# The first microseconds of a two-layer decoder step: memory tokens loaded in two halves, constants loaded later, and the sum of squares moved behind the third key tile

## The chip, the cores and the metric

The kernel runs on one core of one Trainium2 chip. The metric is the device time of one execution in microseconds (us): the median of three runs. TensorE (PE) does the matrix products, ScalarE (ACT) and VectorE (DVE) prepare their operands and read their results, GpSimd (POOL) does some sums, and SyncE (SP) issues most of the loads. The weights are read from device memory as chunks of 128 x 1024 fp32 numbers (512 KB).

## The reference, cut to what matters

One step of a small decoder: a prompt of 256 tokens and 8 samples of 4 tokens (288 token columns in all) go through two layers. Each layer is a recurrent mixer, a cross-attention into 256 memory tokens and a feed-forward part, the last of which has 8 experts. All is in fp32. The piece that the change touches computes the keys and values of the memory tokens:

```
def rms_norm(x, g):
    y = x * rsqrt(mean(x * x, axis=-1) + EPS)
    return y * g

def mem_kv(mem, g, w_k, w_v):          # mem: 256 tokens x 1024 features
    m = rms_norm(mem, g)               # g = norm_memkv[layer]
    k = (m @ w_k).reshape(B, N_MEM, MEM_HEADS, MEM_HD)
    v = (m @ w_v).reshape(B, N_MEM, MEM_HEADS, MEM_HD)
```

## The kernel before, in words

**Tiles.** Activations lie feature-major: 1024 features are `KD` = 8 tiles of 128 partitions, with tokens in the columns. A product of 1024 x 1024 is made of 8 output tiles, each from one weight chunk of eight 128 x 128 blocks. Each fp32 operand is split in two fp32r parts, hi (a copy by ACT) and lo (original minus hi, by DVE), and three matmuls, hi*hi, lo*hi and hi*lo, stand for one product (`mm3`, lines 1773 to 1775). So a key tile of 256 columns is 8 x 3 = 24 matmuls.

**The stream of weights.** SP issues the loads of all chunks in the order in which they are used, into a ring `raw` of 7 places. A place is loaded again once DVE has made the lo part of what was in it (`lo_done`). ACT makes `w_hi` (line 731, in `hi_upto`), DVE makes `w_lo` (line 1137, in `lo_upto`); both have 7 places too, and ACT refills one when PE has finished the group that read it (`full`).

**The order of the work.** `plan()` lists the groups of the whole kernel in order; PSUM's 8 banks go round in that order, so that a group waits until the group that had its bank before has been read by ACT or DVE (`act_freed`, `dve_freed`). The engines' programs are written out by hand in the same order. `AHEAD` says up to which chunk ACT has split weights before it looks at a group.

**The beginning.** SP issues the load of the memory tokens (`memx`, 1 MB), then all small constants (`small`, 984.5 KB: norm weights, convolution weights, identity and other matrices), then three chunks (c0 to c2), the tokens `x_res` (1.2 MB) and four more chunks (c3 to c6). ACT waits for both `memx` and `small`, then multiplies each of the 8 memory tiles with its norm weight (`mem_hi`, line 780), with c0's `w_hi` between them, then makes 8 squares (`memsq`, line 785) and `w_hi` of c1 to c6. DVE makes `mem_lo` (line 1168) and c0's `w_lo`. PE runs key tile 0 on c0, then the group "mem norm" (lines 1820 and 1822): the sum of the squares over the partitions, from `rt`, which POOL adds up from the eight squares (line 2281). Then come key tiles 1 to 7 on c1 to c7, the values (c8 to c15, 192 matmuls of 512 columns, lines 1773 to 1775), and the first mixer's gate products. The factor 1/rms, `rm`, is applied when a key tile is read from PSUM (`kmem`, line 1243), after ACT's root (line 758) and DVE's reciprocal (line 1235). Between key tiles 0 to 3 ACT and DVE make the parts of the second layer's `mem_hi` and `mem_lo` (line 791), between tiles 4 to 7 the squares and parts of the tokens (`h`, `h_hi`, `h_lo`).

## Time and profile before

| | before |
|---|---|
| median of 3 runs | 1945.95 us (1945.78 to 1947.36) |
| span of the profiled execution, first to last instruction | 1944.7 us |
| mean granted TensorE clock in it | 0.973 of full speed |
| PE busy | 1852.8 us, 95% of the span |
| DVE, ACT, POOL busy | 75%, 64%, 10% of the span |
| idle of PE ahead of its first matmul | 14.6 us |
| first chunk's key tile, the idle behind it, "mem norm" | 14.62 to 23.21 us, then 1.73 us |

A row of the timeline gives an instruction's start and duration; consecutive instructions of one kind are merged to one row with their count. PE's matmuls overlap, so what one costs is the distance to the next start, not its duration. A row of the waits gives who idled, what ended the idle time, the total, the number and the longest. "to landing" of a load is the time from its issue to its semaphore. DMA shares are of the core's 16 DMA engines.

### The profile page before, as it was taken

Reading aid. Unit: us, or ns where it says so; the run is one execution under the profiler, and the core shown is the slowest. Engines: PE = TensorE matmul, PEld = TensorE weight load, DVE = VectorE, ACT = ScalarE, POOL = GpSimd, SP = SyncE. Lnnn points to the kernel's source line nnn. Section 1 sums busy time; section 2 is a strip of 40 time slices with the busy share of each in tenths; the row PEclk is TensorE's granted clock in tenths of the full one; section 3 lists DMA queues with packets and bytes.
Section 4 is the critical chain, followed back from the end, with each engine's and each line's share of the span. In section 5 each row is a group of like instructions: output and inputs, shape, how many; then the busy total and the mean of one; then the engine's idle time right before and its main releaser. Section 6 shows DMA issues by size and latency. Waiting matters only on the chain.

```text
span 1944.7 us, 32156 instructions
## 1 busy us (share of the span) xinstructions
PE 1852.8 (95%) x11001; PEld 1601.7 (82%) x11001; DVE 1457.5 (75%) x1765; ACT 1244.2 (64%) x1600; POOL 187.9 (10%) x226
## 2 busy tenths in 40 slices
PE   6998989999899998999999999999999999999994
PEld 6997979999789777978788888888888888888883
DVE  7588456664588568634598988889888898888884
ACT  6576345443476154423687878878788887888873
POOL 3021211000134420201100000000000000000001
PEclk9999999999899999998799999999999999999997
DMA  7646878754443840764799999999999999999993
GB/s 273 227 137 222 327 262 348 268 171 145 155 141 127 310 167 21 277 256 152 281 384 367 380 373 378 360 368 382 372 380 358 374 376 372 383 357 367 381 372 131
DMA packets 150961, 558.35 MB, mean 287 GB/s; under 512 B 16480, under 2 KB 16480, under 8 KB 149424
## 3 DMA queue, kind: packets, MB, share of 16 engines
q1 hardware_dynamic: 139248, 508.71, 70.5%
q10 hardware_dynamic: 6832, 28.44, 3.6%
q0 software_dynamic: 4752, 19.65, 2.8%
q8 instruction: 59, 0.97, 0.2%
q14 instruction: 70, 0.57, 0.1%
HBM read 520.22 MB, written 36.52 MB: 286 GB/s over the span
## 4 chain that ended last, share of the span: by engine, by line
PE 83%; issue 7%; DVE 5%; DMA 2%; ACT 2%; POOL 1%; POOLq 0%; ACTq 0%; DVEq 0%; SPq 0%
PE ps L1773 24%; PE ps L1775 24%; PE ps L1774 24%; DVE w_lo L1137 1%; PE ps L2081 1%; PE ps L2230 1%; DMA raw<-in_stream 1%; PE ps L2208 1%; PE ps L1872 1%; PE ps L1903 1%; DMA y_rows<-ye 1%; PE ps L1894 0%; PE ps L1919 0%; PE ps L2053 0%; ACT w_hi L731 0%
## 5 line engine op out<-in xcount | busy, mean ns | idle before, releaser
L1673 DVE TENSOR_TENSOR w_lo<-raw,w_hi 128x1024 fp32r<-128x1024 f32 x672 | 787.4, 1220 | 49.7 <-ACT w_hi L1062 48.0
L1062 ACT ACTIVATE w_hi<-raw 128x1024 fp32r<-128x1024 f32 x672 | 705.3, 1060 | 142.2 <-PE ps L1775 119.0
L1773 PE MATMUL ps<-w_hi,xe_hi 128*128 128x512 f32 x896 | 358.2, 400 | 4.7 <-DVE w_lo L1673 4.7
L1775 PE MATMUL ps<-w_hi,xe_lo 128*128 128x512 f32 x896 | 354.5, 396 | 0.0
L1774 PE MATMUL ps<-w_lo,xe_hi 128*128 128x512 f32 x896 | 354.0, 395 | 0.0
L731 ACT ACTIVATE w_hi<-raw 128x1024 fp32r<-128x1024 f32 x212 | 220.5, 1051 | 164.3 <-PE ps L1775 109.8
L1137 DVE TENSOR_TENSOR w_lo<-raw,w_hi 128x1024 fp32r<-128x1024 f32 x212 | 266.9, 1268 | 71.7 <-ACT w_hi L731 70.7
L1773 PE MATMUL ps<-h_hi,w_hi 128*128 128x288 f32 x928 | 278.4, 300 | 7.0 <-DVE h_lo L1164 4.2
L1774 PE MATMUL ps<-h_lo,w_hi 128*128 128x288 f32 x928 | 274.5, 296 | 0.0
L1775 PE MATMUL ps<-h_hi,w_lo 128*128 128x288 f32 x928 | 273.6, 295 | 0.0
L1773 PEld LDWEIGHTS ps<-w_hi,xe_hi 128*128 128x128 f32 x896 | 168.9, 189 | 43.0 <-DVE w_lo L1673 5.0
L1775 PEld LDWEIGHTS ps<-w_hi,xe_lo 128*128 128x128 f32 x896 | 168.7, 188 | 40.1
L1774 PEld LDWEIGHTS ps<-w_lo,xe_hi 128*128 128x128 f32 x896 | 169.0, 189 | 38.3
L1773 PEld LDWEIGHTS ps<-h_hi,w_hi 128*128 128x128 f32 x928 | 174.4, 188 | 15.7 <-issue 14.1
L1773 PE MATMUL ps<-w_hi,gt_hi 128*128 128x512 f32 x448 | 178.1, 398 | 0.0
L1775 PE MATMUL ps<-w_hi,gt_lo 128*128 128x512 f32 x448 | 176.9, 395 | 0.0
L1774 PE MATMUL ps<-w_lo,gt_hi 128*128 128x512 f32 x448 | 176.9, 395 | 0.0
L1775 PEld LDWEIGHTS ps<-h_hi,w_lo 128*128 128x128 f32 x928 | 175.4, 189 | 0.0
L1774 PEld LDWEIGHTS ps<-h_lo,w_hi 128*128 128x128 f32 x928 | 175.0, 189 | 0.3
L1775 PEld LDWEIGHTS ps<-w_hi,gt_lo 128*128 128x128 f32 x448 | 84.2, 188 | 20.0
L1774 PEld LDWEIGHTS ps<-w_lo,gt_hi 128*128 128x128 f32 x448 | 84.3, 188 | 19.4
L1773 PEld LDWEIGHTS ps<-w_hi,gt_hi 128*128 128x128 f32 x448 | 84.2, 188 | 19.3
(411 smaller groups left out, 2551.3 us busy)
## 6 DMA issues: line engine op xcount, KB each, us to landing
raw<-in_experts SPq DMA_DIRECT2D x672, 512.0 KB, 5.5
raw<-in_stream SPq DMA_DIRECT2D x253, 512.0 KB, 4.5
rest<-in_stream SPq DMA_DIRECT2D x28, 512.0 KB, 7.3
x_rows<-zeros ACTq DMA_DIRECT2D x1, 13824.0 KB, 59.6
out_ssd_s<-s_new ACTq DMA_DIRECT2D x16, 512.0 KB, 6.8
y_rows<-ye POOLq DMA_DIRECT2D x9, 512.0 KB, 7.2
home<-in_stream SPq DMA_DIRECT2D x8, 512.0 KB, 7.5
xs<-x_rows POOLq DMA_DIRECT2D x8, 512.0 KB, 4.7
```

What stands on the lines that cost most here:

```text
L731: act.activation(w_hi[:, o % HL, :], landing_place(k), ACT.Copy).then_inc(hi_done, 1)
L1062: act.activation(w_hi[:, (NSPLIT + p) % HL, :], raw[:, slot, :], ACT.Copy) \
L1137: dve.tensor_tensor(w_lo[:, o % HL, :], landing_place(k), w_hi[:, o % HL, :].bitcast(F32), ALU.subtract).then_inc(lo_done, 1)
L1673: dve.tensor_tensor(w_lo[:, (NSPLIT + p) % HL, :], raw[:, (NRING + p) % RAW, :], w_hi[:, (NSPLIT + p) % HL, :].bitcast(F32), ALU.subtract) \
L1773: pe.matmul(out, l_hi, r_hi, start=start, stop=False)
L1774: pe.matmul(out, l_hi, r_lo, start=False, stop=False)
L1775: return pe.matmul(out, l_lo, r_hi, start=False, stop=stop)
L1872: a = pe.matmul(out[:, tt * NMEM:(tt + 1) * NMEM], q[:, j, tt * P:(tt + 1) * P], kt[:, j, :], start=(dd == 0), stop=(dd == 1))
L1903: a = pe.matmul(out, vt[:, m, j * P:(j + 1) * P], prt[:, m, j // 2, :], start=(m == 0), stop=(m == 1))
L2081: a = pe.matmul(out[:, j * n:(j + 1) * n], adt_s[half][0:n, tt, 4 * hb + j:4 * hb + j + 1].broadcast_to([n, n]), tri_r[:, :], start=(j == ...
L2208: a = pe.matmul(ps[:, j // 4, (j % 4) * P:(j % 4 + 1) * P], htok[0:n, m, j * P:(j + 1) * P], sel0[0:n, m, :], start=(m == 0), stop=(m == 2))
L2230: a = pe.transpose(ps[:, 4, k * P:(k + 1) * P], ge[:, f % 2, k * P:(k + 1) * P], ident)
```

## The change

- The memory tokens and the norm weights of their keys and values, which were a part of `small`, are now one input array. It is loaded in two halves: the weights of both layers with memory tiles 0 to 3, and tiles 4 to 7.
- SP's order is now: first half, c0, second half, c1, c2, `small`, c3, `x_res`, c4 to c6.
- ACT runs a square root of one column at its very start, behind a memset by DVE. The table of functions for the root is so loaded before anything has landed; the activations Identity, Square and Copy are in it too.
- ACT no longer waits for `small` ahead of the memory tiles. c0's `w_hi` comes behind memory tile 0 (it came behind tile 3), and c1's behind tile 7 (it came behind the squares). DVE makes c0's `w_lo` behind tile 0 (it came behind tile 4), and c1's behind tile 5.
- PE runs "mem norm" behind key tile 2, not 0. It is the third place later in `plan()` too, which moves it two banks on, and lets ACT split c7 and c8 ahead of the root, and DVE c6 and c7 ahead of the reciprocal.
- `small` is 16 columns shorter, so that all buffers that lie behind it start 64 bytes earlier.

The core of the diff:

```
-for _name, _n in [("g_mix", 16), ("g_mem", 16), ("g_memkv", 16), ("g_ffn", 16),
+for _name, _n in [("g_mix", 16), ("g_mem", 16), ("g_ffn", 16),
...
+NORM_BEHIND = 3
...
-    p = second(memory(0), "mem norm")
+    first = memory(0)
+    p = first[:NORM_BEHIND] + [("mem norm", "act", 0)] + first[NORM_BEHIND:]
...
-            sp.dma_start(memx[:, :, :], t["mem"]).then_inc(mem_in, 16)
-            sp.dma_start(small[:, :], t["small"]).then_inc(small_in, 16)
+            sp.dma_start(memx_g[:, 0:MEM_HALF], t["mem"][:, 0:MEM_HALF]).then_inc(mem_in[0], 16)
...
+                if i == 0:
+                    sp.dma_start(memx_g[:, MEM_HALF:], t["mem"][:, MEM_HALF:]).then_inc(mem_in[1], 16)
                 if i == 2:
+                    sp.dma_start(small[:, :], t["small"]).then_inc(small_in, 16)
+                if i == 3:
                     sp.dma_start(x[:, :, :], t["x"]).then_inc(x_in, 16)
...
-            act.wait_ge(mem_in, 16)
-            act.wait_ge(small_in, 16)
+            act.wait_ge(warm, 1)
+            act.activation(rmt[:, 0:1], rm[:, 0:1], ACT.Sqrt)
+            act.wait_ge(mem_in[0], 16)
             for j in range(KD):
+                if j == 1:
+                    hi_upto(1)
+                if j == KD // 2:
+                    act.wait_ge(mem_in[1], 16)
                 act.activation(mem_hi[0][:, j, :], memx[:, j, :], ACT.Identity,
-                               scale=gains("g_memkv", 0)[:, j:j + 1]).then_inc(hh_done, 1)
-                if j == 3:
-                    hi_upto(1)
+                               scale=mem_gains(0)[:, j:j + 1]).then_inc(hh_done, 1)
+            hi_upto(2)
             for j in range(KD):
                 act.activation(memsq[:, j, :], memx[:, j, :], ACT.Square).then_inc(sq_done, 1)
+            act.wait_ge(small_in, 16)
             root("mem norm", rmt, NMEM + 2)
...
-            dve.wait_ge(small_in, 16)
+            dve.memset(rm[:, 0:1], 1.0).then_inc(warm, 1)
             for j in range(KD):
-                scaled_lo(mem_lo[0], memx, gains("g_memkv", 0), mem_hi[0], j, j + 1)
-                if j == 4:
+                scaled_lo(mem_lo[0], memx, mem_gains(0), mem_hi[0], j, j + 1)
+                if j == 0:
                     lo_upto(1)
+                if j == 5:
+                    lo_upto(2)
+            dve.wait_ge(small_in, 16)
             act_read("mem norm")
...
-                    if l == 0 and j == 0:
+                    if l == 0 and j == NORM_BEHIND - 1:
+                        pe.wait_ge(small_in, 16)
                         out = open_group("mem norm", NMEM + 2)
                         pe.wait_ge(acc_done, KD - 1)
...
-            pe.wait_ge(small_in, 16)
             keys(0, range(KD))
```

What SP issues first. Before, and then in the changed kernel (`memx_g` is the array with the norm weights in its first 16 columns):

```order
L661 DMA memx<-in_mem 128x2048
L662 DMA small<-in_small 128x1969
L695 DMA raw<-in_stream 128x1024 x3
L697 DMA x_res<-in_x 128x2304
L695 DMA raw<-in_stream 128x1024 x4
```

```order
L670 DMA memx_g<-in_mem 128x1040
L703 DMA raw<-in_stream 128x1024
L705 DMA memx_g<-in_mem 128x1024
L703 DMA raw<-in_stream 128x1024 x2
L707 DMA small<-in_small 128x1953
L703 DMA raw<-in_stream 128x1024
L709 DMA x_res<-in_x 128x2304
L703 DMA raw<-in_stream 128x1024 x3
```

The constants moved from the second place to behind c2, and c0 from the third to the second, behind half the memory.

What ACT runs first, up to the root of the norm. Before, and then changed (`landed0` is the semaphore of the ring's first place):

```order
L780 ACT_TABLE_LOAD [waits small_in]
L780 ACTIVATE mem_hi_72<-memx,small 128x256 [waits mem_in]
L780 ACTIVATE mem_hi_72<-memx,small 128x256 x3
L731 ACTIVATE w_hi<-raw 128x1024 [waits landed0]
L780 ACTIVATE mem_hi_72<-memx,small 128x256 x4
L785 ACTIVATE memsq<-memx 128x256 x8
L731 ACTIVATE w_hi<-raw 128x1024 [waits landed1]
...
L758 ACT_TABLE_LOAD
L758 ACTIVATE rmt<-ps,small 128x258 [waits full]
```

```order
L790 ACT_TABLE_LOAD
L790 ACTIVATE rmt<-rm 128x1 [waits warm]
L797 ACTIVATE mem_hi_72<-memx_g 128x256 [waits mem_in0]
L743 ACTIVATE w_hi<-raw 128x1024 [waits landed0]
L797 ACTIVATE mem_hi_72<-memx_g 128x256 x3
L797 ACTIVATE mem_hi_72<-memx_g 128x256 [waits mem_in1]
L797 ACTIVATE mem_hi_72<-memx_g 128x256 x3
L743 ACTIVATE w_hi<-raw 128x1024 [waits landed1]
L801 ACTIVATE memsq<-memx_g 128x256 x8
L743 ACTIVATE w_hi<-raw 128x1024 [waits landed2,small_in]
...
L743 ACTIVATE w_hi<-raw 128x1024 [waits full,landed0]
L743 ACTIVATE w_hi<-raw 128x1024 [waits full,landed1]
```

Two table loads became one that waits for nothing, the split of c0 moved ahead by three tiles and that of c1 ahead of the squares, and two more splits (c7 and c8, the last two rows) stand ahead of the root, which follows them.

What DVE runs up to the reciprocal. Before, and then changed:

```order
L1168 SCALAR_TENSOR_TENSOR mem_lo_74<-memx,small,mem_hi_72 128x256 [waits hh_done,small_in]
L1168 SCALAR_TENSOR_TENSOR mem_lo_74<-memx,small,mem_hi_72 128x256 [waits hh_done] x4
L1137 TENSOR_TENSOR w_lo<-raw,w_hi 128x1024 [waits hi_done]
L1168 SCALAR_TENSOR_TENSOR mem_lo_74<-memx,small,mem_hi_72 128x256 [waits hh_done] x3
L1137 TENSOR_TENSOR w_lo<-raw,w_hi 128x1024 [waits hi_done] x5
L1235 RECIPROCAL rm<-rmt 128x258 [waits act_freed]
```

```order
L1246 MEMSET rm 128x1
L1185 SCALAR_TENSOR_TENSOR mem_lo_74<-memx_g,mem_hi_72 128x256 [waits hh_done]
L1154 TENSOR_TENSOR w_lo<-raw,w_hi 128x1024 [waits hi_done]
L1185 SCALAR_TENSOR_TENSOR mem_lo_74<-memx_g,mem_hi_72 128x256 [waits hh_done] x5
L1154 TENSOR_TENSOR w_lo<-raw,w_hi 128x1024 [waits hi_done]
L1185 SCALAR_TENSOR_TENSOR mem_lo_74<-memx_g,mem_hi_72 128x256 [waits hh_done] x2
L1154 TENSOR_TENSOR w_lo<-raw,w_hi 128x1024 [waits hi_done,small_in]
L1154 TENSOR_TENSOR w_lo<-raw,w_hi 128x1024 [waits hi_done] x5
L1255 RECIPROCAL rm<-rmt 128x258 [waits act_freed]
```

c0's `w_lo` moved ahead by four tiles; c1's stands between tiles 5 and 6 of `mem_lo`; the wait for the constants stands behind them all, and eight chunks are split ahead of the reciprocal, not six. From the fourth key tile on, and on all engines, the rows of the two kernels are the same but for their line numbers, the name of the memory's array and the bank waits of two groups of the values.

## Rows read from the trace of the kernel before

**Rows 1.** The page, its first line

```profile
span 1944.7 us, 32156 instructions
```

**Rows 2.** Waits of PE, whole span: total us, times, longest

```profile
PE ps L1820 <- POOL rt L2281: 3.8, 1, 3.8
```

**Rows 3.** The chain that ended last, first 15 us: start, us, what

```profile
1.44 7.02 DMA small<-in_small
...
8.53 1.28 ACT L780
...
9.82 1.70 ACT mem_hi L780 x4
```

**Rows 4.** Windows: us, busy (x) of PE, PEld, DVE, ACT, POOL; clock, DMA, GB/s

```profile
14.60:18.60 4.00, 3.98 (x19) 4.00 (x20) 3.17 (x4) 4.00 (x10) 3.26 (x5) 1.00 1.03 411
...
26.00:28.70 2.70, 2.70 (x14) 2.70 (x14) 2.66 (x5) 2.13 (x4) 0.00 (x0) 0.50 0.93 278
...
30.00:47.00 17.00, 17.00 (x143) 17.00 (x143) 14.94 (x24) 13.88 (x26) 6.90 (x7) 1.00 0.53 174
```

**Rows 5.** Loads with KB, us to landing: memory, chunk c0

```profile
memx<-in_mem SPq DMA_DIRECT2D x1, 1024.0 KB, 4.8
...
raw<-in_stream SPq DMA_DIRECT2D x1, 512.0 KB, 7.8
```

**Rows 6.** Timeline of SP and ACT from the start: start, us, engine, line

```profile
0.99 0.39 SPq L661 DMA_DIRECT2D memx<-in_mem  x1
...
1.91 1.68 SPq L695 DMA_DIRECT2D raw<-in_stream  x3
...
11.43 1.04 ACT L731 ACTIVATE w_hi<-raw 128x1024 fp32r<-128x1024 f32 x1
...
13.97 2.55 ACT L785 ACTIVATE memsq<-memx 128x256 f32<-128x256 f32 x8
16.42 5.78 ACT L731 ACTIVATE w_hi<-raw 128x1024 fp32r<-128x1024 f32 x6
```

**Rows 7.** Timeline of DVE, 10 to 28 us

```profile
13.31 1.22 DVE L1137 TENSOR_TENSOR w_lo<-raw,w_hi 128x1024 fp32r<-128x1024 f32 x1
14.44 2.23 DVE L1168 SCALAR_TENSOR_TENSOR mem_lo<-memx,small,mem_hi 128x256 fp32r<-128x256 f32 x3
17.50 7.87 DVE L1137 TENSOR_TENSOR w_lo<-raw,w_hi 128x1024 fp32r<-128x1024 f32 x5 [0.83 <-ACT w_hi L731]
25.63 1.77 DVE L1235 RECIPROCAL rm<-rmt 128x258 f32<-128x258 f32 x1 [0.25 <-ACT rmt L758]
```

**Rows 8.** Timeline of PE: first matmul, norm, tile 1, values, gate

```profile
14.62 0.55 PE L1773 MATMUL ps<-mem_hi,w_hi 128*128 128x256 f32 x1 [14.62 <-DVE w_lo L1137]
...
23.21 1.22 PE L1820 MATMUL ps<-rt,small 128*128 128x256 f32 x2 [3.75 <-POOL rt L2281]
...
24.94 0.56 PE L1773 MATMUL ps<-mem_hi,w_hi 128*128 128x256 f32 x1
...
46.86 0.40 PE L1773 MATMUL ps<-w_hi,mem_hi 128*128 128x512 f32 x1
...
68.65 0.29 PE L1773 MATMUL ps<-h_hi,w_hi 128*128 128x288 f32 x1
```

**Rows 9.** Timeline of POOL: the sum of squares of the memory

```profile
14.76 0.75 POOL L2281 TENSOR_TENSOR rt<-memsq 128x256 f32<-128x256 f32 x1 [14.06 <-ACT memsq L785]
15.66 7.50 POOL L2281 TENSOR_TENSOR rt<-rt,memsq 128x256 f32<-128x256 f32 x6
```

**Rows 10.** Timeline of DVE, key tile 5's step, beside POOL's second sum

```profile
41.30 0.42 DVE L1243 TENSOR_TENSOR kmem<-ps,rm 128x256 f32<-128x256 f32 x1 [0.47 <-PE ps L1775]
41.64 1.56 DVE L1168 SCALAR_TENSOR_TENSOR h_lo<-x_res,small,h_hi 128x288 fp32r<-128x288 f32 x2
43.12 1.83 DVE L1137 TENSOR_TENSOR w_lo<-raw,w_hi 128x1024 fp32r<-128x1024 f32 x1
```

**Rows 11.** Window of the experts, columns as in rows 4

```profile
1100.00:1944.00 844.00, 818.91 (x3658) 663.35 (x3656) 728.81 (x674) 664.77 (x694) 12.54 (x19) 0.99 0.95 358
```

More of the change, by code:

```diff
@@ L306, in build_program @@
         assert dt_off + 2880 <= end, (dt_off + 2880, end)
-        memx = at("memx", [KD, NMEM], F32, S[5])
+        memx_g = at("memx_g", [2 * KD + KD * NMEM], F32, S[5])
+        memx = memx_g[:, 2 * KD:].rearrange("p (k n) -> p k n", n=NMEM)
+        MEM_HALF = 2 * KD + KD // 2 * NMEM
         memsq = at("memsq", [KD, NMEM], F32, S[3])
@@ L450, in build_program @@
         x_in = sem("x_in")
-        mem_in = sem("mem_in")
+        mem_in = [sem(f"mem_in{i}") for i in range(2)]
+        warm = sem("warm")
         prev_in = sem("prev_in")
@@ L634, in landing_place, with mem_gains @@
             return rest[:, n, :] if kind == "split" else raw[:, n % RAW, :]
+        def mem_gains(l):
+            return memx_g[:, l * KD:(l + 1) * KD]
         def bank(g, n=512, rows=P):
@@ L791, in _ @@
                         act.activation(mem_hi[1][:, k, :], memx[:, k, :], ACT.Identity,
-                                       scale=gains("g_memkv", 1)[:, k:k + 1]).then_inc(hh_done, 1)
+                                       scale=mem_gains(1)[:, k:k + 1]).then_inc(hh_done, 1)
                 else:
@@ L1226, in conv_tile @@
                                          ALU.mult, ALU.add).then_inc(done, 1)
+            dve.memset(rm[:, 0:1], 1.0).then_inc(warm, 1)
+            for j in range(KD):
+                scaled_lo(mem_lo[0], memx, mem_gains(0), mem_hi[0], j, j + 1)
+                if j == 0:
+                    lo_upto(1)
+                if j == 5:
+                    lo_upto(2)
             dve.wait_ge(small_in, 16)
-            for j in range(KD):
-                scaled_lo(mem_lo[0], memx, gains("g_memkv", 0), mem_hi[0], j, j + 1)
-                if j == 4:
-                    lo_upto(1)
             act_read("mem norm")
@@ L1248, in _ @@
                     if j < 4:
-                        scaled_lo(mem_lo[1], memx, gains("g_memkv", 1), mem_hi[1], k, KD + k + 1)
+                        scaled_lo(mem_lo[1], memx, mem_gains(1), mem_hi[1], k, KD + k + 1)
                     else:
@@ L2473, in small_inputs @@
     put("g_mem", gains(a["norm_mem"]))
-    put("g_memkv", gains(a["norm_memkv"]))
     put("g_ffn", gains(a["norm_ffn"]))
@@ L2592 @@
         "x": feature_major(np.concatenate([a["x_prompt"][0], a["x_sample"].reshape(NB * TS, D)])),
-        "mem": feature_major(a["mem_prompt"][0]),
+        "mem": np.ascontiguousarray(np.concatenate(
+            [a["norm_memkv"].reshape(2 * KD, P).T, feature_major(a["mem_prompt"][0]).reshape(P, KD * NMEM)], 1)),
         "g_fin": np.ascontiguousarray(np.broadcast_to(a["norm_final"][None], (P, D))),
```

## The prediction

> **What bounds the kernel now.** I read the waits of PE first. Over the whole span PE works nearly all the time, and the change touches only its beginning, so the question is what PE waits for there. Two waits stand out: the first matmul starts at 14.62 us, after c0's lo part [rows 8], and "mem norm" waits 3.8 us for POOL's sum of squares [rows 2]. Then the chain of waits tells what lies ahead of 14.62: the constants land at 1.44 + 7.02 = 8.46 us, the table load takes 1.28, ACT's memory tiles follow from 9.82 [rows 3], c0 is split at 11.43 by ACT [rows 6] and at 13.31 by DVE [rows 7]. c0 itself had landed at 1.91 + 7.8 = 9.7 us [rows 5, 6]. So the start hangs on the constants, on a table and on an order of ACT and DVE, not on the weights. Behind the second wait there is a third cost, which no wait shows. PE's clock fell in the idle time: between 26.0 and 28.7 us it is granted 0.50 (1.2 GHz), and 14 matmuls start in 2.7 us, one in 0.19 to 0.21; from 30 to 47 us it is 1.00 (2.4 GHz), and 143 start in 17 us, one in 0.119 [rows 4]. In the first 4 us of work the row shows 1.00 but 19 matmuls in 4.0 us [rows 4]: the pace, 0.21, is that of the lower level, and I go by the pace. A key tile of 24 matmuls takes 24 x 0.119 = 2.86 us at the upper level. The values start at 46.86 us [rows 8]; that is the mark by which I measure the head start.
>
> **The loads.** The memory's 1.05 MB, issued at 0.99, landed 4.8 us later, at 5.8 [rows 5, 6], and the queue moves 411 GB/s while it is full [rows 4]. The transfers came one behind the other: the constants' 1.01 MB would add 2.5 us to 5.8, and landed at 8.46; c0 another 1.3, and landed at 9.7. In the new order, with 1.3 us for each 0.52 MB: first half at 4.5 us, c0 at 5.9 (a tenth added, as both rows above came a tenth or two late), second half 7.2, c1 8.5, c2 9.7, constants 12.2, c3 13.5, the tokens 16.4, c4 17.7, c5 18.9, c6 20.2. c7 and c8 are issued as c0 and c1 are done with, while the queue is still full, and land at 21.5 and 22.8. Nothing is added or removed but one issue by SP (0.4 us, ahead of c1, which has over 6 us until it lands: nothing). The Trainium skill (DMA: Bandwidth & Descriptors, section Specifications) gives a limit of about 358 GB/s from device memory per core. By it the first half and c0, 1.06 MB, would come 0.4 us later than at 411, and the head start would be 0.4 us shorter; the trace has 411 and does not agree, and I go by the trace.
>
> **Table load and start of PE.** The table load (1.28 us [rows 3]) waits only for the engines' start, and with DVE's memset and one activation of one column (bounds: nothing, and the 0.5 us of a whole memory tile) is over by about 3 us, ahead of 4.5. I take nothing. Where the load is gone from at 22 us it lay beside POOL's sum: nothing too. ACT does memory tile 0 at 4.6, waits for c0 (5.9), and splits it in 1.04 us [rows 6]. DVE follows with 1.22 [rows 7], free since 5.5: lo part done at 8.2, PE starts at 8.3 us. Before, 14.62. **Gain 6.3.**
>
> **Tile 0.** PE then needs the memory tiles' lo parts. ACT resumes at 6.9, a tile each 0.40 us (four from 9.82 to 11.43 [rows 3, 6]), the second half has landed, and tile 7 is done at 9.8. DVE takes tiles 1 to 5 from 8.1 to 10.2, a tile each 0.42, while PE uses one in 3 x 0.21 = 0.63 us: no wait up to tile 5, whose matmuls end at 8.3 + 18 x 0.21 = 12.1. But now c1's lo part stands ahead of tiles 6 and 7. ACT splits c1 from 9.7 to 10.8, and makes the squares from 10.7. POOL begins its sum at about 11.4, and beside POOL DVE is slower: three memory tiles took 2.23 us, 0.74 each, with one of them at the undisturbed pace [rows 7], so up to 0.9 each; five weight splits took 7.87, 1.57 each instead of 1.22 [rows 7]. So c1's lo part is done at 12.3, tile 6 at 13.1 and tile 7 at 14.0. PE waits 1.0 and 0.5 us and ends tile 0 at 14.5: 6.2 us for what took 23.21 - 3.75 - 14.62 = 4.8 [rows 8]. **Loss 1.4.** The bounds: without POOL's slowing tile 7 is there at 12.9 and the loss is 0.3; with a fully slowed c1 (1.8 us, as in [rows 10]) it is 1.9. I take 1.4, which is nearest to the rows.
>
> **The wait of 3.75 us.** POOL's seven additions took 14.76 to 23.16, 8.4 us [rows 9]. From 11.4 that is 19.8 at the latest. PE runs tiles 1 and 2 first, 14.5 + 2 x 2.86 = 20.2. c1's parts are there at 12.3; c2's at 15.9, since ACT's eight squares end at 13.1 (2.55 us [rows 6]) and its split and DVE's take 1.0 and 1.7; needed at 17.4. The constants, which PE, ACT and DVE now await ahead of the norm, land at 12.2: ACT is behind its squares until 13.1, so a margin of 0.9 us. The wait goes to nothing, with 0.4 us to spare: **gain 3.8** (bounds 3.4 and 3.8).
>
> **The clock behind it.** Without the idle time PE stays at the upper level. "mem norm", 23.21 to 24.94, takes half of 1.73: **gain 0.9**. Tile 1 ended six tiles ahead of 46.86, at 46.86 - 6 x 2.86 = 29.7, so it took 4.8 us from 24.94; now 2.86: **gain 1.9**. Without the clock's return in time the two are nothing, and tiles 1 and 2 cost up to 2 us each more.
>
> **Tiles 3 to 7 and the values.** c3 to c7 are split by ACT as they land (c4 17.7, c5 18.9, c6 20.2, c7 21.5) and by DVE 2.2 to 3 us behind: 20, 21.5, 22.7, 23.9 for c4 to c7. PE needs c4 at 24.0, c5 at 26.8, c7 at 32.5. The root on ACT is now behind the split of c8 (landed 22.8, done 23.8), so it ends at 24.2, and DVE's reciprocal (1.77 us [rows 7]) at 26.0. Before, that ended at 27.4 with one key tile done; now it has five behind it. So DVE starts reading key tiles with a backlog. A step of DVE takes some 2.4 us, and beside POOL's second sum 44.88 - 41.30 = 3.6 us (0.34 + 1.48 + 1.76 by the starts [rows 10]). By these, c8's lo part is done at 30.7, c9's 33, c10's 37, c11's 40.5, c12's 43.5. The values take them from 35.4 on, one in 2.7 us (eight from 46.86 to 68.65 before [rows 8]): c11 at 43.6, c12 at 46.3. The margin is 2.8 us at the least, so I cost the backlog at nothing. The banks too: tile 7 needs tile 0's bank read (26.4, against 32.5). Everything behind starts from landings, semaphores and ring places that move along with PE.
>
> **The sum.** 6.3 - 1.4 + 3.8 + 0.9 + 1.9 = 11.5; walked along PE: 14.5, 20.2, norm until 21.1, five tiles until 35.4, against 46.86: 11.4. The profiled span, 1944.7 [rows 1], becomes 1933.3. The median of the runs lies 1.25 us above that span, so I predict **1934.5 us**.
>
> **The rivals.**
> *DVE is not slowed (a larger gain).* Tiles 6 and 7 come at the undisturbed pace, and the loads land a little earlier: 12.4 to 13 us, 1933.3. For it: POOL's first additions are short and DVE may slip between them. Against: 2.23 us for three tiles.
> *The clock comes late.* PE's start has now two holes of 1.0 and 0.5 us in it. In the profile it reached the upper pace about 4 us after its unbroken start, and 5.5 us after 23.21. If it comes only at some 18 us, tile 1 and a part of tile 2 run at half pace: 1.8 us lost, up to 3.5 if it takes the tile behind too; 1936.3 to 1938.
> *The loads don't come one by one.* If the first half and c0 share the queue with what is behind, c0 lands 1 to 3 us later and so does PE's start: 1937. This is also the case in which the change doesn't do what it says. The Trainium skill (DMA: Bandwidth & Descriptors, section Queues, rings and completion order) says that completion is not FIFO per issuing engine, which would speak for it. The landings 5.8, 8.46 and 9.7, in the order of issue and spaced by their sizes, speak against.
> *Given back in the values.* If DVE is beside POOL in all of tiles 0 to 7, four more steps cost 1.2 each, c11's lo part comes at 45.3, and PE waits 1.7 us there; 9.7 of the gain stay. That alone is still faster; only if the backlog grows by some 10 us is the gain within 0.2%, 1943, and the chance below is for that.
> *Slower.* The experts' stretch, 844 us at a DMA share of 0.95 and PE at 97% [rows 11], is close to both limits. The buffers behind the constants lie 64 bytes lower, the experts' operands among them. If that made each of the 672 expert chunks dearer by over (11.4 + 3.9) / 672 = 0.023 us, the kernel would be slower by over 0.2%; at 0.03 us, 1955. Nothing in the rows says that an address counts.
>
> **How the numbers follow.** Forecast 0.60; larger gain 0.10; clock late 0.14; loads not one by one 0.07; given back 0.06; slower 0.03. About 0.2%, 3.9 us, is what can be told from no change. The first four are all faster by more: 0.91; given back is the same: 0.06; slower 0.03. The range reaches from the larger gain, with half a us for the runs' spread, to the late clock: 1932.6 to 1938.5. It leaves out the end of the late loads, the fifth and the sixth case, some 0.15.
>
> **What would show it.** In the profile after: first matmul at 8.3 us and the last of the eight memory tiles' matmuls at 14.5; no wait on POOL ahead of the norm; granted clock 1.00 and a pace of 0.119 from tile 1 on; the values from 35.4 us; every later mark, the experts' start too, 11 us earlier. The steps are wrong if c0 lands after 7 us, if tile 6 does not wait, if tile 1 is at 0.21, or if DVE's lo parts end PE's waits in the values.

## The result: 0.5% faster, and the profile after

| | before | after |
|---|---|---|
| median | 1948.87 us (22 runs) | 1943.89 us (22 runs) |
| ratio of the runs, 95% interval | | 0.9948 (0.993 to 0.9965) |
| profiled execution, its span | 1945.95, 1944.7 us | 1929.92, 1928.3 us |
| mean granted clock in it | 0.973 | 0.977 |
| executions below 1940 us | 0 | 7 |
| executions from 1940 to 1951 us | 17 | 13 |
| executions from 1951 to 1961 us | 5 | 1 |

The change is faster, as forecast, but by 5 us, not by 11.5, and the median lies outside the range. (Five executions took from 2073 to 3684 us and are left out of all that is sorted and counted below: one of after, one of experiment 10, and three of before taken beside experiments 8 to 11; without its one, after's median is 1943.63.) The medians alone mislead. Sorted, the executions of each kernel fall into two groups. Before: 17 from 1945.8 to 1950.9 (median 1948.5), 5 from 1956.7 to 1960.7 (1958.1). After: 7 from 1929.9 to 1937.5 (1935.4), 14 from 1942.2 to 1951.2 (1945.4). Group against group the gain is 13.1 and 12.7 us. The medians are only 5 us apart since before's lies in its lower group and after's in its upper one. The three runs on which the prediction stood were all of before's lower group.

**The beginning.** First, what PE waits for in the first 60 us of after (total us, times, longest):

```profile
PE ps L1793 <- DVE w_lo L1154: 8.5, 1, 8.5
PE ps L1793 <- DVE mem_lo L1185: 1.1, 2, 0.9
```

The start and two short holes are all. The wait of [rows 2] on POOL is gone. Then the landings of the first 20 us (KB, us from issue to landing), the memory's two halves and the constants, and the piece of the chain of waits that is c0's load:

```profile
memx_g<-in_mem SPq DMA_DIRECT2D x1, 520.0 KB, 3.9
memx_g<-in_mem SPq DMA_DIRECT2D x1, 512.0 KB, 5.9
small<-in_small SPq DMA_DIRECT2D x1, 976.5 KB, 9.2
...
1.44 4.72 DMA raw<-in_stream
```

With their issues (0.99, 1.90 and 3.52 us) they landed at 4.9, 7.8 and 12.7 us, and c0 at 6.2: one behind the other, in the order of issue, each 0.3 to 0.6 us later than forecast. The timeline of ACT and DVE up to the reciprocal, and of POOL's sum, which answers to [rows 6, 7, 9] (start, duration, engine, line, [idle before, released by]):

```profile
0.99 1.28 ACT L790 ACT_TABLE_LOAD   x1 [0.99 <-PEq L2618]
2.29 0.20 ACT L790 ACTIVATE rmt<-rm 128x1 f32<-128x1 f32 x1
4.89 0.51 ACT L797 ACTIVATE mem_hi<-memx_g 128x256 fp32r<-128x256 f32 x1 [2.40 <-DMA memx_g<-in_mem]
6.17 1.06 ACT L743 ACTIVATE w_hi<-raw 128x1024 fp32r<-128x1024 f32 x1 [0.77 <-DMA raw<-in_stream]
...
7.26 1.23 DVE L1154 TENSOR_TENSOR w_lo<-raw,w_hi 128x1024 fp32r<-128x1024 f32 x1 [1.34 <-ACT w_hi L743]
...
11.01 1.22 DVE L1154 TENSOR_TENSOR w_lo<-raw,w_hi 128x1024 fp32r<-128x1024 f32 x1 [0.54 <-ACT w_hi L743]
12.15 1.83 DVE L1185 SCALAR_TENSOR_TENSOR mem_lo<-memx_g,mem_hi 128x256 fp32r<-128x256 f32 x2
...
11.67 1.14 POOL L2301 TENSOR_TENSOR rt<-memsq 128x256 f32<-128x256 f32 x1 [10.97 <-ACT memsq L801]
12.96 6.79 POOL L2301 TENSOR_TENSOR rt<-rt,memsq 128x256 f32<-128x256 f32 x6
```

The table is loaded and the root run by 2.5 us, beside the loads. c0 is split as it lands. The two memory tiles beside POOL take 1.83 us, 0.92 each. POOL ends at 19.75. PE's timeline, which answers to [rows 8]:

```profile
8.54 0.58 PE L1793 MATMUL ps<-mem_hi,w_hi 128*128 128x256 f32 x1 [8.54 <-DVE w_lo L1154]
...
13.15 0.39 PE L1793 MATMUL ps<-mem_hi,w_hi 128*128 128x256 f32 x1 [0.85 <-DVE mem_lo L1185]
...
14.04 0.38 PE L1793 MATMUL ps<-mem_hi,w_hi 128*128 128x256 f32 x1 [0.26 <-DVE mem_lo L1185]
...
14.48 0.28 PE L1793 MATMUL ps<-mem_hi,w_hi 128*128 128x256 f32 x1
...
19.92 0.64 PE L1841 MATMUL ps<-rt,small 128*128 128x256 f32 x2
...
20.77 0.36 PE L1793 MATMUL ps<-mem_hi,w_hi 128*128 128x256 f32 x1
...
34.47 0.39 PE L1793 MATMUL ps<-w_hi,mem_hi 128*128 128x512 f32 x1
```

First matmul at 8.54, tile 1 at 14.48, norm at 19.92 without a wait, values at 34.47 against 46.86 [rows 8]. The head start is 12.4 us, forecast 11.4. So the beginning did what was predicted, and the missing microseconds had to be sought far behind it.

### The profile page after: what moved, and what is told of

Read it like the earlier page. It is cut to its first block, busy times and chain, and to the rows that moved or that the text cites. A ratio compares the mean times of both kernels' runs of the same rounds, so it can differ in the third digit from the quotient of the medians.

```text
span 1928.3 us, 32159 instructions
## 1 busy us (share of the span) xinstructions
PE 1842.7 (96%) x11001; PEld 1589.5 (82%) x11001; DVE 1456.7 (76%) x1766; ACT 1243.0 (64%) x1600; POOL 187.2 (10%) x226
## 4 chain that ended last, share of the span: by engine, by line
PE 82%; issue 7%; DVE 5%; DMA 3%; ACT 2%; POOL 0%; POOLq 0%; ACTq 0%; DVEq 0%; SPq 0%
PE ps L1793 24%; PE ps L1794 24%; PE ps L1795 24%; DVE w_lo L1154 1%; PE ps L2250 1%; PE ps L2101 1%; DMA raw<-in_stream 1%; PE ps L2228 1%; PE ps L1892 1%; PE ps L1923 1%; DMA out_ssd_s<-s_new 1%; DMA y_rows<-ye 1%; PE ps L1914 0%; ACT w_hi L743 0%; PE ps L1939 0%
```

## The experiments

In all profiles the mark is the start of the values, the first matmul with 512 columns. A head start is its distance from before's 46.86.

**1. The changed kernel again (a_again).** No edit.

> The changed kernel, unaltered, once more, to see in which stretches an execution of about 1944 us differs from the profiled one of 1929.9. Theory 1 (the head start of 11.4 us is real and is carried to the end; what varies between executions is how long TensorE is granted the lower clock later on): executions come in two groups some 11 us apart, near 1933 and near 1945, with mean granted clocks near 0.976 and 0.970; in a profile of the upper group the values start at 35 us as in the fast one, and the lost time lies in one or two stretches of granted 0.50 behind 800 us. Rival 1 (the head start itself is lost in some executions, by late loads or a late clock in the first key tiles): in a profile of the upper group the values start near 46 us, and the later stretches are alike. Rival 2 (the experts' chunks take longer in some executions, from the 64 bytes): the stretch of the experts is longer at a clock of 1.00.

Nine runs: five from 1931.5 to 1935.3 and four from 1942.5 to 1948.9; ratio 0.9917 (0.9887 to 0.9947). The profile taken was this time of the upper group, span 1947.3 at a clock of 0.968. Its beginning is nearly that of after (values at 36.13, a head start of 10.7), and yet it ends 19 us later than after's. The two groups are of one and the same kernel, and the difference is not made at the beginning. There a_again shows one thing that after doesn't, POOL's sum and the norm:

```profile
13.19 7.71 POOL L2301 TENSOR_TENSOR rt<-rt,memsq 128x256 f32<-128x256 f32 x6
...
21.05 0.67 PE L1841 MATMUL ps<-rt,small 128*128 128x256 f32 x2 [0.72 <-POOL rt L2301]
```

The six additions took 7.71 us, not 6.79, and PE waits 0.72 us for them. In the later profiles with the changed beginning they took 7.5 to 7.8, and PE waited 0.5 to 0.7 where it had not waited longer already; after's is the exception. The last addition makes the difference. In after it started at 19.01, just ahead of VectorE's split of c3 (19.20), and took 0.74 us. In a_again that split came first, at 19.09, and the addition, from 19.23, took 1.67:

```profile
L2301 POOL TENSOR_TENSOR rt<-rt,memsq x1: 1672/1672/1672, 19.2 to 19.2; 128x256 f32<-128x256 f32 x1
```

Theory 1 of the expectation holds but for the place: the lost time lies near 690 us, not behind 800 (see "Where the groups part").

**2. The first load held back (a_late).** SP waits for a memset by DVE of 2048 columns ahead of its first load:

```
+            sp.wait_ge(held, 1)
...
+            dve.memset(kmem[0][:, :, :], 0.0).then_inc(held, 1)
```

> The changed kernel with the first load held back by a memset of one 128 x 2048 tile on VectorE, 1 to 2.5 us, so that everything behind starts later by d and nothing else changes. Theory 1 in the form that the later clock losses depend on when idle times fall, counted from the start: the two groups shift by d only, but the share of executions in the upper group changes from that of the unaltered kernel (14 of 21). Rival 1 and 2: the groups shift by d, and the share stays. If the groups are d later and the share is the same within what 5 rounds can tell, the theory of timing from the start is not supported.

```profile
10.87 0.58 PE L1796 MATMUL ps<-mem_hi,w_hi 128*128 128x256 f32 x1 [10.87 <-DVE w_lo L1156]
...
37.70 0.39 PE L1796 MATMUL ps<-w_hi,mem_hi 128*128 128x512 f32 x1
```

PE's timeline: first matmul 2.3 us later than in after, values at 37.70, which is 1.6 later than in a_again. Twelve runs: 1937.43, ten of them from 1934.8 to 1940.5 with a median of 1937.1. That is 1.8 above after's lower group and 3.7 above that of a_again, measured beside it. Inside a group a later start is carried to the end, as far as such scatter lets one say. Only two of the twelve were in the upper group, against four of nine in a_again; so few executions don't settle whether the start's time sets the share.

**3. The sum behind tile 0 again (a_norm1).**

```
-NORM_BEHIND = 3
+NORM_BEHIND = 1
```

> The changed kernel with the norm's sum back behind the first key tile; loads, table and split orders stay. By the steps of the prediction PE starts at 8.5 us and ends tile 0 at 14.5, then waits for POOL until 19.8 (5.3 us, longer than before, since the start moved by 6.1 and the sum by only 3.1), the clock falls, the norm takes 1.7 and tile 1 up to 4.8: the values start at about 19.8 + 1.7 + 4.8 + 17.2 = 43.5 us, 3.4 earlier than before, 8 later than in the changed kernel. So 1945 in the lower and 1953 in the upper group if theory 1 holds and the clock falls; if the clock does not fall in that wait, 41 us and 2 us less. Rival 1: no difference to the changed kernel beyond its scatter.

```profile
20.92 1.19 PE L1841 MATMUL ps<-rt,small 128*128 128x256 f32 x2 [6.15 <-POOL rt L2301]
...
43.44 0.39 PE L1793 MATMUL ps<-w_hi,mem_hi 128*128 128x512 f32 x1
...
16.00:26.20 10.20, 5.28 (x23) 5.13 (x24) 7.18 (x7) 6.18 (x9) 4.35 (x4) 0.50 1.03 411
```

Two rows of PE's timeline and one window (columns as in [rows 4]): PE waits 6.15 us for POOL, the clock is at 0.50 for the 10.2 us from 16.0, and the values start at 43.44, a head start of 3.4. So of the 10.7 us of a_again, 7.3 hang on the new place of the sum. Without it most of the earlier start goes into a longer wait for POOL. Twelve runs: 1952.96, ratio 0.9994 (0.9968 to 1.002), so the rest of the change alone does not move the median. Four are from 1940.1 to 1944.7 (median 1941.6, expected 1945), eight from 1950.9 to 1956.8 (1955.6, expected 1953). Against before's groups measured beside it, 1948.1 and 1958.8, they gain 6.5 and 3.2 us; the head start of 3.4 fits the second and not the first.

**4. Only the sum moved, in the kernel before (b_norm3).**

```
+NORM_BEHIND = 3
...
-    p = second(memory(0), "mem norm")
+    first = memory(0)
+    p = first[:NORM_BEHIND] + [("mem norm", "act", 0)] + first[NORM_BEHIND:]
...
-                    if l == 0 and j == 0:
+                    if l == 0 and j == NORM_BEHIND - 1:
```

> The kernel before with only the norm's sum moved behind key tile 2 (plan and PE); loads, table and splits as before. By the steps of the prediction: PE starts at 14.6, tile 0 takes 4.8, tiles 1 and 2 run at the upper clock (5.8), the norm 0.9 and five tiles 14.3: the values start at 40.4 instead of 46.9 us, a head start of 6.5. With the 3.4 that the start alone gave this makes 9.9 of the 12 of the whole change; the rest is the tile 1 that neither alone frees. Fast half of the executions near 1941.5, the other near 1952. The rival that the norm's wait was only a part of a slower supply of weights gives under 3 us, since c1 to c6 would then be late.

```profile
14.56 0.55 PE L1776 MATMUL ps<-mem_hi,w_hi 128*128 128x256 f32 x1 [14.56 <-DVE w_lo L1140]
...
25.09 0.59 PE L1823 MATMUL ps<-rt,small 128*128 128x256 f32 x2
...
40.36 0.40 PE L1776 MATMUL ps<-w_hi,mem_hi 128*128 128x512 f32 x1
```

PE starts as in before, does not wait for POOL, and the values start at 40.36: a head start of 6.5, which is the prediction's 3.8 + 0.9 + 1.9 to 0.1. Twelve runs: 1944.76; eight in the lower group, median 1941.6 against 1948.9 for before's lower group measured beside it, 7.3 us. The rest of the head start of 10.7 to 12.4, some 4 to 6 us, comes with the earlier loads and splits.

**Where the groups part.** Both kernels run the same matmuls, so one can ask when the same one starts. The 4600th starts at 653.0 us in before's profile, at 635.4 in after's and at 637.6 in a_again's; the 5200th at 734.9, 715.9 and 734.3. So a_again has lost 14.7 of its 15.4 us between these two. (Matmul 8000, among the experts, starts at 1247.2, 1229.0 and 1248.1.) The stretch is the recurrent mixer of the second layer, with many small matmuls of 128 columns. PE there waits for DVE's mask `mt` (line 1554 of before, 1574 of after) before the first product of mask and tokens, called the first y tile below. Its timeline row in a_again, the 27 us from there, and the y tile in after:

```profile
688.90 1.00 PE L2130 MATMUL ps<-mt,xt 128*64 128x128 f32 x8 [3.45 <-DVE mt L1574]
...
689.30:716.30 27.00, 26.45 (x128) 20.78 (x125) 8.42 (x23) 6.90 (x22) 0.00 (x0) 0.50 0.13 52
...
682.37 0.66 PE L2130 MATMUL ps<-mt,xt 128*64 128x128 f32 x8 [0.65 <-DVE mt L1574]
```

In a_again PE idles 3.45 us and its clock is down behind it for 27 us. (Another 3.4 us are lost just ahead, where PE waits 4.0 us for the last gate chunk, that is the weights of the mixer's last gate tile.) The first suspect was a write of the recurrent state, which took 9.47 us in a_again, 6.73 in after, and kept that chunk waiting.

**5. The state's writes cut short (a_noout).** The sixteen writes move 8 of 1024 columns each.

```
-                    act.dma_start(t["out_ssd_s"][b, half], s_new[k][:, :]).then_inc(state_out[k], 16)
+                    act.dma_start(t["out_ssd_s"][b, half][:, 0:8], s_new[k][:, 0:8]).then_inc(state_out[k], 16)
```

> The changed kernel, but of each of the 16 state writes of the samples (512 KB each, in the stretch 600 to 670 us) only 8 of 1024 columns are written, so that output is not complete. Theory A: the executions fall in two groups because one of these writes comes late behind the weights' loads (9.5 us against 6.4 and 6.7 in the fast profile), VectorE's last state and the split behind it come late, PE idles 4.3 instead of 1.5 us before its last gate tile and 3.7 before the first y tile, and the clock stays at half for 27 us. Without the writes the upper group is gone: at most 1 of 12 executions more than 6 us above the lowest, and the lower group is faster by the waits that go, 2 to 10 us. Rival B: the upper group comes from the low load of PE in that stage whatever the writes do: 4 to 8 of 12 in the upper group still.

The output is so left incomplete. Eight runs, all from 1940.5 to 1944.9, with the upper group's mean clock of 0.968 to 0.970. From the waits of PE in 640 to 760 us, one window of a_noout, and the window of after that answers to it:

```profile
PE ps L2130 <- DVE mt L1574: 4.0, 2, 3.4
...
682.30:709.30 27.00, 26.45 (x130) 20.93 (x131) 8.75 (x23) 6.90 (x22) 0.00 (x0) 0.50 0.08 30
...
683.00:710.00 27.00, 25.97 (x230) 22.35 (x230) 14.81 (x30) 13.20 (x39) 3.62 (x1) 1.00 0.08 32
```

The late write is not the cause: without it PE idles 3.4 us ahead of the first y tile, and 130 matmuls are done in 27 us at 0.50. In after's profile 230 are done in such 27 us, at 1.00.

**6. Idle matmuls at the two places (a_fill).** 24 matmuls of 128 columns, whose result is overwritten, ahead of the last gate chunk and as many ahead of the first y tile:

```
+            def busy(out):
+                for _ in range(24):
+                    pe.matmul(out[:, 0:P], ident_r[:, :], future_r[:, :], start=True, stop=True)
...
+                if key == ("z", KI - 1):
+                    busy(out)
...
+                    if (tt, hb) == (0, 0):
+                        busy(out)
```

> The changed kernel with 24 idle matmuls (128 columns, into a bank that the group has just claimed and overwrites) before PE waits for the weights of the last gate tile, and 24 before it waits for the first y tile's mask, 2.7 us each at the upper clock. If the idle of PE at these two places makes the clock fall (theory A and B both), they keep PE at work and the upper group shrinks to at most 2 of 12, at a cost of 0 to 3 us in the lower group: median 1934 to 1938 against some 1940 of the changed kernel. If the group is made elsewhere: 4 to 8 of 12 in the upper one, and 0 to 3 us slower in both.

Six runs from 1932.0 to 1937.3, median 1935.77, ratio 0.9891 (0.9859 to 0.9922). The upper group is gone. But the idle matmuls are not free. Behind the experts PE turns the tokens; a_fill's rows, then after's:

```profile
1909.50 4.00 PE L2293 MATMUL ps<-small,x_res 128*128 128x128 f32 x18 [2.75 <-issue]
...
1899.70 2.84 PE L2285 MATMUL ps<-small,x_res 128*128 128x128 f32 x24 [0.57 <-issue]
```

In all five profiles with idle matmuls at both places PE waits 2.1 to 4.4 us in all at this point, for nothing that the profile shows, and falls 3.7 to 5.9 us behind there; in the nine others it waits at most 0.7. Why 48 instructions, 1200 us earlier, do this, no run tells.

**7. The kernel before, unaltered (b_again).**

> The kernel before, unaltered, for a second profile. Executions near 1948 and near 1958, in about equal parts. If this one is of the upper group: the same long idle of PE (over 3 us) at the last gate tile or the first y tile and a low clock of over 20 us behind it, so that the two groups are no work of the change. If its low clocks are elsewhere, that theory falls for this kernel.

Eight runs: 1957.21; six from 1955.8 to 1959.6, and the profile, span 1957.5, is one of them. So before has the same upper group, and now one kernel's two kinds can be laid side by side. Windows of 691 to 697.8 and 701 to 728 us, first before's profile, then b_again's:

```profile
691.00:697.80 6.80, 6.80 (x28) 5.30 (x29) 4.77 (x6) 2.48 (x4) 1.30 (x1) 0.50 0.89 340
701.00:728.00 27.00, 25.89 (x226) 22.16 (x226) 15.76 (x32) 14.35 (x44) 3.63 (x1) 1.00 0.11 42
...
691.00:697.80 6.80, 6.02 (x48) 5.26 (x49) 4.87 (x6) 3.42 (x6) 1.73 (x1) 1.00 0.96 359
701.00:728.00 27.00, 26.10 (x129) 20.99 (x130) 9.17 (x24) 6.97 (x24) 0.00 (x0) 0.50 0.12 46
```

The timelines of the first y tile, before's and b_again's, and of DVE ahead of it in b_again:

```profile
701.44 0.66 PE L2110 MATMUL ps<-mt,xt 128*64 128x128 f32 x8
...
701.35 1.12 PE L2110 MATMUL ps<-mt,xt 128*64 128x128 f32 x8 [2.26 <-DVE mt L1554]
...
694.76 4.63 DVE L1137 TENSOR_TENSOR w_lo<-raw,w_hi 128x1024 fp32r<-128x1024 f32 x4
```

The y tile starts at the same time in both, 701.4, since DVE sets it: four chunks' lo parts in a row, then the mask. What differs is PE. In before's profile the clock was down from 691.0 to 697.8, PE did 28 matmuls where b_again did 48, and came to the y tile just in time, with no idle before it. Behind it the clock stayed up. In b_again the clock was up, PE was early, idled 2.26 us (over 3 were expected), and the clock went down for 27 us. By these two profiles a short fall ahead of the wait spares the long one behind it. One further ahead does not: a_again's clock was down from 668.6 to 675.4 us and PE still idled 3.45. The long fall costs (226 - 129) matmuls at 226 in 27 us, 11.6 us; the groups of before are 10 to 13 apart. Over all profiles without idle matmuls, the three of the upper group have 2.26, 3.45 and 3.44 us of idle time ahead of the first y tile and the 27 us behind it, the five of the lower one at most 0.65 and no such fall.

**8 and 9. The idle matmuls in both kernels (b_fill, a_fill_again).** The same edit in the kernel before, and a_fill again beside it.

> The kernel before with the same 48 idle matmuls as a_fill: 24 before the weights of the last gate tile, 24 before the first y tile's mask. Theory C (the change brings 11 to 14 us in every execution; the two groups of executions are made by PE's idle before the first y tile, in both kernels alike): nearly all executions are in the lower group, 1946 to 1950, and this kernel lies 12 to 14 us above the changed kernel with the same matmuls. Rival D (the change itself makes the upper group more frequent, and the matmuls only mend the change): the kernel before keeps its share of four in ten above 1953 and its median is not moved.

> The changed kernel with the 48 idle matmuls, once more, on the same chip as the kernel before with them. Theory C: 1932 to 1938, at most one execution in ten above 1941. Chance (the six low executions of the first run were luck; with a share of a half that is one in 64): 3 or more of 9 above 1941.

Values' start, b_fill and a_fill_again:

```profile
47.29 0.40 PE L1777 MATMUL ps<-w_hi,mem_hi 128*128 128x512 f32 x1
...
35.91 0.40 PE L1797 MATMUL ps<-w_hi,mem_hi 128*128 128x512 f32 x1
```

b_fill: twelve runs from 1942.0 to 1950.8, median 1946.69. a_fill_again: seven, 1934.77 (with experiment 6, thirteen runs: 1935.33). Neither has an upper group (one run, 1942.83, lies at its edge). The head start is 47.29 - 35.91 = 11.4, and the medians differ by 11.9 (11.4 with all thirteen). With the second group taken out of both kernels, the change brings what the prediction said. (Both pay for the idle matmuls at their end; expected were 12 to 14.) Over all runs, the changed kernel with idle matmuls ahead of the y tile (experiments 6 and 9 to 12) had none of 33 executions in the upper group, the kernel before with them none of 12; without them it was 18 of 30 and 45 of 110. As many instructions at another place were not tried.

**10. Idle matmuls ahead of the y tile alone (a_fill_y).** Only the second of the two places.

> The changed kernel with only the 24 idle matmuls before the first y tile's mask. If the idle there alone (3.7 and 2.5 us in the profiles of the upper group, under 1 in the lower) lets the clock fall, the lower group is all there is, as with both, and up to 1.5 us faster than a_fill, since the last gate tile isn't held up. If the gate tile's idle counts too, 2 or more of 9 above 1941.

Six runs from 1933.4 to 1938.2, median 1937.01. The one place is enough to remove the upper group, so the idle ahead of the y tile is what matters. Up to 1.5 us less than a_fill was expected; the median is 2.2 above a_fill_again's, measured beside it, although the late wait of a_fill is not there. These runs don't tell what the matmuls ahead of the gate chunk are worth.

**11. c1 split behind memory tile 7 (a_order).** On top of a_fill:

```
-                if j == 5:
-                    lo_upto(2)
+            lo_upto(2)
```

> The changed kernel with the 48 idle matmuls, and VectorE splits c1 behind memory tile 7 and not behind tile 5. The prediction put 1.0 and 0.5 us of PE's idle in key tile 0 down to that split. Then tiles 6 and 7 are there at 10.4 to 11.4 us, PE has no wait in tile 0 (0.85 and 0.26 in the profile) and ends it at 13.2 to 13.5 instead of 14.5; c1's lo part comes at 12.9, in time. Head start of the values 1 us larger, median 1 us below a_fill. If the split isn't the cause (POOL's sum slows the memory tiles anyway), tile 0 ends at 14.5 again or tile 1 waits for what tile 0 gained.

```profile
PE ps L1846 <- POOL rt L2308: 1.9, 1, 1.9
```

From the waits of PE in the first 60 us. The holes in tile 0 are gone, as expected: it ends at 13.2 us. But the norm starts at 21.29, against 20.82 in a_fill_again, since POOL's sum ends 0.5 us later, as much as the whole of this profile is late from the first matmul on (9.03 against 8.55). What PE gained in tile 0 it spends waiting, 1.9 us instead of 0.5, and behind the longer wait its clock is at 0.50 from 22.4 to 25.8. The values start at 37.91, 2.0 behind a_fill_again: 0.5 from the start, 1.5 from the clock. Median 1937.92, where 1 us below a_fill was expected: 3.2 above a_fill_again. The time lost in tile 0 (1.1 us, booked at 1.4) is no loss while POOL's sum stands behind it, and without it the longer wait brought the clock down.

**12. The 64 bytes given back (a_pad).** Before and after differ in pace where neither waits. a_pad is a_fill with 16 unused columns at the end of the constants, so that every buffer behind them lies where it lies in before:

```
-                  ("lower", 64), ("ebase", 8), ("eps", 1), ("first", 128), ("iota", 128)]:
+                  ("lower", 64), ("ebase", 8), ("eps", 1), ("first", 128), ("iota", 128), ("pad", 16)]:
```

> The version of a_fill with 16 unused columns added to the end of the constants' array, so that every buffer behind it lies at the address that it has in the kernel before (64 bytes higher than in the changed kernel). Nothing else differs; the load of the constants moves 8 KB more. In the profiles so far the matmuls 2000 to 3500 (the first layer's feed-forward) took 203.8 us in the three profiles with before's addresses and 200.6 in the four with the changed ones, and the matmuls 8000 to 10000 (experts) 449.5 and 450.4. Theory D, the address sets it: 2000 to 3500 takes 203.8 again, 8000 to 10000 takes 449.5, the head start at the values stays (start at 35 to 36 us), and the median is some 1 us above a_fill's 1935.3, about 1936. Rival, the earlier arrival in the stream or the other order of the beginning sets it: 200.6 and 450.4 stay, and the median stays at 1935.

The same 1500 matmuls of the first feed-forward, 900 and then 600, in before and in after; the 600 in a_late; the 900 in a_pad:

```profile
306.70:426.70 120.00, 120.00 (x902) 120.00 (x901) 77.22 (x113) 52.51 (x77) 0.00 (x0) 1.00 0.74 278
426.70:510.50 83.80, 81.79 (x602) 81.55 (x601) 36.59 (x43) 28.66 (x36) 7.49 (x6) 0.98 0.47 153
...
292.50:411.50 119.00, 119.00 (x902) 119.00 (x902) 77.26 (x113) 52.54 (x77) 0.00 (x0) 1.00 0.74 280
411.50:493.10 81.60, 79.58 (x602) 79.35 (x602) 36.52 (x43) 28.60 (x36) 7.46 (x6) 1.00 0.48 156
...
415.50:498.60 83.10, 81.08 (x601) 80.85 (x601) 36.51 (x43) 28.61 (x36) 7.46 (x6) 0.98 0.48 154
...
294.90:414.90 120.00, 120.00 (x902) 120.00 (x902) 77.08 (x113) 52.48 (x77) 0.00 (x0) 1.00 0.73 278
```

And with the same 2000 matmuls of the experts, before, after, a_pad:

```profile
1247.20:1696.70 449.50, 449.50 (x2001) 364.27 (x2000) 397.39 (x366) 366.17 (x378) 4.31 (x8) 1.00 0.98 373
...
1229.00:1679.40 450.40, 450.40 (x2001) 363.81 (x2001) 397.84 (x366) 366.20 (x378) 4.29 (x8) 1.00 0.98 372
...
1221.80:1671.40 449.60, 449.60 (x2001) 364.08 (x2000) 396.47 (x365) 365.50 (x378) 4.30 (x8) 1.00 0.98 371
```

The first 900 take 120.0, 119.0 and again 120.0 us, the experts' 2000 take 449.5, 450.4 and again 449.6. This pace goes with the address, not with the order of the beginning: in all profiles the 900 take 120.0 with before's addresses (five) and 119.0 with the changed ones (nine). But it is only 1.7 of the 3.2 us by which the 1500 matmuls are faster in after. The other 1.5 is TensorE's clock, down for 3.4 us at 441.8 us in before, behind an idle time of 2.0 us, and not down in after behind the same idle time. The expectation overlooked that two changed kernels, a_late and a_fill_y, have this fall too and take 202.1 us. All five profiles with before's addresses have it and two of the nine others, so a tie to the address is possible but not shown. The experts give back 0.9 us in 2000 matmuls, some 1.8 in 4000, so that the two paces alone nearly cancel. Values at 36.13, eight runs from 1934.4 to 1941.4, median 1937.89: 2.6 above a_fill's, where 1 was expected and a_fill's two medians differ by 1.0. The stretches above don't account for 2.6.

## Why the prediction was wrong, point by point

**Loads, table and start of PE: right.** 8.54 us against 8.3. The loads came in order. The rival in which they don't, and for which the Trainium skill (DMA: Bandwidth & Descriptors, section Queues, rings and completion order) would have spoken, is not borne out by the landings 4.9, 6.2 and 7.8; the Trainium skill's rule says only that the order is not promised, which no run here contradicts.

**Tile 0: right.** Waits of 0.85 and 0.26 us, forecast 1.0 and 0.5; end at 14.48, forecast 14.5. It took 5.9 us against 4.8, a loss of 1.1 booked at 1.4. The cause is as told, c1's split and POOL beside DVE: with the split moved, in a_order, the waits are gone.

**The wait on POOL: right but for 0.5 us.** In after's profile POOL ended at 19.75 (forecast 19.8) and PE was there at 19.9. But that profile is the fastest. In the others the additions took 9.0 us from the first's start to the last's end, not the 8.4 taken over from [rows 9], and ended between 20.6 and 21.1 where nothing was held back, so that PE waited 0.5 to 0.7 us. The 8.4 are no constant: they depend on which of DVE's instructions the additions fall beside, and the order of these had changed. b_norm3, whose wait is nothing, gives this and the next step together: 6.5 against 6.6 forecast.

**The clock: right.** From tile 1 on the pace was that of the upper level, and the two holes in tile 0 did not bring it down; the rival "the clock comes late" did not occur. Tiles 1 and 2 took 19.92 - 14.48 = 5.44 us for 48 matmuls, 0.113 each and not 0.119, and tiles 3 to 7 took 34.47 - 20.77 = 13.70, not 14.3, which is why its values were 0.9 us early. The 0.119 belongs to before's addresses: tiles 3 to 7 take 13.71 us in a_fill and 14.48 in a_pad, which differ in nothing but the 16 columns. (a_again and a_fill_again take 14.2, between the two, so the address is not all.) In a_again, a_fill, a_fill_again and a_pad they start at 35.7 to 36.1, forecast 35.4.

**DVE's backlog: right.** The reciprocal ended at 24.68 + 1.77 = 26.45 (forecast 26.0), and PE waited for nothing in the values.

**The median as a base: wrong.** "The median of the runs lies 1.25 us above that span" took three executions of before for its time. They were all of the lower group. Measured again beside the experiments, before had medians from 1948.9 to 1957.2, as the groups happened to mix.

**"Everything behind starts from landings, semaphores and ring places that move along with PE": wrong.** Between 640 and 735 us it depends on where TensorE's clock happens to fall, and this doesn't move along: before's profile and b_again's, of one kernel, differ in it. The head start is there in both of after's groups, but the lower one and the upper one are 10 to 13 us apart, as large as the gain itself. The sign that the prediction named, the experts' start 11 us earlier, shows it: matmul 8000 starts 18.2 us earlier than before's in after's profile and 0.9 us later in a_again's. After had 18 of 30 executions in the upper group, before 45 of 110 (counted above 1954 us). Whether the change makes it likelier stays open: the shares vary as much between kernels of one kind, 4 of 9 in a_again, 2 of 12 in a_late, 6 of 8 in b_again. So the failed step is one term that the sum lacks, 0 or some 11 us at the y tile. With it the forecast would have had two values, 1934.5 and some 1945; measured medians of the groups are 1935.4 and 1945.4. The range lacked the second.

**The 64 bytes: named, but one-sided.** "Nothing in the rows says that an address counts" was true of the rows and false of the chip. It gave a small chance to a loss alone. Measured are both signs: 1.7 us gained in the 1500 matmuls of the feed-forward, 0.3 to 0.8 in key tiles 3 to 7, 0.9 lost in 2000 of the experts'. The gain inside a group, 12.7 to 13.1, exceeds the head start of 10.7 to 12.4 by up to 2.4 us. What makes that up is open: addresses, short falls of the clock such as the one at 441.8 us, and the scatter of the runs are all of this size.

## What to carry to other kernels

A wait costs its length only while the clock stays up behind it. Look in the profile for waits ahead of stages of small matmuls with a low granted clock behind them; here waits of 2.3 to 3.5 us had it. Idle matmuls put into such a wait removed the loss of 11.6 us (a_fill: 1935.3 us over 13 runs, against 1943.9 for the changed kernel, whose lower group alone has 1935.4). Look at the rest of the profile after it too: at two places together they cost 4 to 6 us at the kernel's end. Sort the single executions before you trust a median; two groups at a distance like that of the gain make any forecast from one profile a forecast of one group. And where a sum is made by a slow engine, give PE other tiles to do first: that alone was 6.5 us of a head start of 10.7 to 12.4.

## What was unexpected of the hardware

- After an idle time of 2.3 to 3.5 us TensorE was granted 0.50 for 27 us, though PE was busy 26.1 of 27.0 us [in the window of b_again above]. Each of the 14 profiles, of either group, has another such stretch between 899 and 961 us, 20 to 38 us long; in after it is the 27.3 us from 902.5 on, with PE busy for 21.6 of them. The Trainium skill (TensorE: Matmul & The Clock Gate, section What's actually happening) says that the watching block does not restart with the kernel, so that the same kernel's changes of clock come at different places. b_again and before bear this out: one kernel, and at 691 us one is at 0.50 and the other at 1.00. The same section of the Trainium skill puts the ramp at less than 1% of a typical span. The fall at the y tile is no ramp at a kernel's start, but its 11.6 us of 1950, 0.6%, are within that share too, and yet as much as the whole gain.
- Buffers moved by 64 bytes changed the pace of matmuls by 5% in key tiles 3 to 7 (13.71 us in a_fill, 14.48 in a_pad), by 0.8% in the feed-forward (119.0 and 120.0 us), and by 0.2% the other way in the experts (450.4 and 449.6). Which operand it is, and by what mechanism, no run here tells.
- VectorE and GpSimd slow each other, both ways: two memory tiles of DVE took 1.83 us beside POOL's first additions, and POOL's seven took 8.8 to 9.0 us in most profiles of the changed beginning, 8.25 in before [rows 9] and 7.9 in after's one. A single addition took 0.74 us where it started ahead of a weight split of DVE, and 1.67 where the split had started first (after and a_again above).
